# Doubling steps through four corners of the array, and every third low half of the projection's weights by GpSimd

## The chip, the cores and the metric

The kernel runs on one core of one Trainium2 chip. The metric is the device time of one execution in microseconds, as the median of several runs. The profile was taken of one more execution, and all rows below are from it.

## The reference, cut to what matters

One layer of an encoder on 256 tokens of width 2048, in float32. `h = rms_norm(x)` is projected by `w_in` (2048 x 7296) into the inputs of three mixers; their outputs go through `w_out`, then follows an MLP with `w_up` and `w_down` (width 8192). The mixer that the change touches is the RWKV-7 one, 12 heads of width 64 in two directions:

```
z = h @ w_in                       # 57 tiles of 128 columns
...
state = state * w + sa (x) bb + v (x) k      # one step per token, forward and backward
y = state . r
```

The kernel computes this recurrence in 4 chunks of 64 tokens. Within a chunk it needs the inverse of a 64 x 64 triangular matrix I - A for each head, direction and chunk. It builds the inverse by doubling: blocks of size 1 are joined to blocks of size 2, then 4, 8, 16, 32 and 64. One level computes P = A Z (masked to the blocks off the diagonal) and then Z + Z P.

## The kernel before, in words

**The float32 matmuls.** Each weight half (128 x 1024 floats, 512 KB) is fetched by SyncE into `raw` (a ring of 4, `fetch(h)`), rounded by ScalarE into `w_hi` (`hi(h)`, L1066), and VectorE takes the rest, `w_lo = raw - w_hi` (`lo(h)`, L614; both rings have 3 places). TensorE multiplies three times (L1398: hi x hi, L1399: hi x lo, L1400: lo x hi). Eight "depths" (one depth is these three matmuls of 128 x 256) use up one half; the projection has 912 depths and 114 halves. `fetch(h)` waits until the low half h-4 is done; `lo(h)` waits for `hi(h)` and for the matmuls of half h-3.

**The order of the work.** The RWKV mixer runs in 6 turns (a turn is a pair of heads). Each engine writes out the same sequence, `stage_a`: `products` (5 gaps), then five levels (`level(t, p, n, ...)`, 2 gaps each), so 15 gaps in a turn. Into each gap go the next 5 or 6 depths of the projection on TensorE (`DONE` lists how many depths are done before each gap), and on ScalarE and VectorE the halves that come due by the same list: `hi(h)` 2 depths and `lo(h)` 5 depths after the place in the ring is wanted back. The turns hold depths 336 to 840. Steps of the turn before (`chunk`) and preparations of the turn behind (`feed`, `tilde`) are threaded in between: `steps`, `between`, `behind`.

**A level.** Two directions d = 0 and 1, four chunks m, two heads e. The heads lie on partitions 0 to 63 and 64 to 127. `make_p(d)` does 8 matmuls of 64 x 64 into bank 4 + d (L1502), `make_q(d)` 8 more (L1514). Each matmul is two instructions in the trace, so `make_p(0)` and `make_p(1)` together are "x32", and so are the two `make_q`; I call such 32 instructions a block. Each matmul takes its operands from head e's partitions and writes to the same partitions, so a block uses two corners of the array, those on its diagonal. VectorE answers `make_p` with `take_p` (L763, mask into `p1s`) and `make_q` with `take_q` (L772, add into `zd`) and `transposed` (L653, into `zt`). In each level `make_p(d)` waits for `zd_ready` of its direction, and `make_q(d)` for `zt_ready` and `p1_ready` of its.

**The small steps that the rows name.** L1569 and L1577 are the four and four matmuls of `chunk`'s `u()`: the first four write to the partitions that they read from (the corners on the diagonal), the second four write to the other head's partitions (the other two corners). L1424 is the `lora` product. L1458 are `key_products` at a turn's start, which need the banks that L716 reads. L660 to L662 normalise `kkn` (`between` of level 1). L694 to L701 are `queries` and `keys`; L678 to L686 are `sums`.

**GpSimd in the turns.** It has no gaps. In turns 0 to 4 it does `bonus_and_keys` (from level 2 on): for d = 0 L516 and L519, then for d = 1 L516, and L519 only after VectorE's `keys(0)` (it waits for `tilde_ready`, L701), then L523 and L524. In each turn but the first it does `decay_state` twice (L545). Later it squares the MLP's activations (L570).

Of the kernel before, what the change touches and what calls it, by code (L numbers as in the profile page):

```python
# [8 lines left out]
ALU = mybir.AluOpType  # L9
ACT = mybir.ActivationFunctionType  # L10
F32 = mybir.dt.float32
# [4 lines left out]
T = 256  # L16
# [13 lines left out]
C = 64  # L30
NC = T // C
# [62 lines left out]
LAST_GAP = len(DONE) - 2  # L94
HI_LAG, LO_LAG, DRAIN_LAG, SHIFT_LAG = 2, 5, 2, 6


# [73 lines left out]
def layer(nc, x, pre_mix_g, w_in, na_rpb, rw_mu_prev, rw_mu_next, rw_w0, rw_w2, rw_a0, rw_a2, rw_k_k, rw_k_a,  # L171
          rw_r_k, rw_g2, rw_lnx_g, rw_lnx_b, w_out, post_mix_g, pre_mlp_g, w_up, w_down, post_mlp_g,
          cst_d, late_d, decay_d, out):
    with ExitStack() as ctx:
# [124 lines left out]
        def late_const(name):  # L299
# [31 lines left out]
            "vec_t", "vec_ready", "coef_ready",  # L331
            "hi_half", "lo_half", "gemm_half", "bank_free", "pad_free", "zs_ready",
            "lora_done", "lora_free", "wd_ready", "quarter_done", "kk_sqd", "kk_summed", "kk_root", "kk_ready",
# [21 lines left out]
        def run(pieces):  # L355
            for piece in pieces:
                piece()
# [76 lines left out]
        def _(sp):  # L434
# [18 lines left out]
            def fetch(h):  # L453
                if h >= RAW:
                    sp.wait_ge(s["lo_half"], h - RAW + 1)
# [45 lines left out]
        def _(pool):  # L501
# [4 lines left out]
            pool.dma_start(a2s, rw_a2.rearrange("l d r c -> (l d r) c")).then_inc(s["lora_in"], 16)  # L506

            def feed(t):
                return [nothing] * 5
# [17 lines left out]
            def products(t, p, steps):  # L527
                if t == RW_CT - 1:
                    pool.wait_ge(s["kb_ready"], 2 * RW_CT)
                    pool.wait_ge(s["tilde_ready"], 2 * RW_CT)  # L530
                    pool.dma_start(g2s, rw_g2[0]).then_inc(s["g2_in"], 16)
                run(steps)

            def level(t, p, n, steps, between, behind):
                run(steps)
                run(between)
                run(behind)

# [9 lines left out]

            stage_a(nothing, feed, tilde, products, level, chunk, STARTS)

# [23 lines left out]
        def _(dve):  # L574
# [64 lines left out]
            def gap():  # L639

                done = DONE[at["gap"]]
                while at["shift"] < RW_GROUPS and KT * (group_tiles(at["shift"])[-1] + 1) + SHIFT_LAG <= done:
                    shift(at["shift"])
                    at["shift"] += 1
                while at["lo"] < OUT_H and (at["gap"] == LAST_GAP or HALF_KT * (at["lo"] - SPLIT + 1) + LO_LAG <= done):
                    lo(at["lo"])
# [59 lines left out]
            def products(t, p, steps):  # L706
# [14 lines left out]
                def first_inverse(d):  # L721
                    dve.wait_ge(s["bm_ready"], 4 * t + (2 * d + 2))
                    for e in range(2):
                        h = slice(e * C, e * C + C)
                        last = dve.tensor_tensor(p1s[h, d * NC:(d + 1) * NC],
                                                 bms[p][h, (2 * d + e) * NC:(2 * d + e + 1) * NC, h],
                                                 off[h, 0].unsqueeze(1).broadcast_to([C, NC, C]), ALU.mult)
# [5 lines left out]
                    transposed(zd, zt, d, "zd_ready")  # L733

# [23 lines left out]
            def level(t, p, n, steps, between, behind):  # L758
# [8 lines left out]
                def take_q(d):  # L767
# [3 lines left out]
                    if n < len(LEVELS) - 1:  # L771
                        dve.tensor_tensor(zd[:, half], q_ps, zd[:, half], ALU.add).then_inc(s["zd_ready"], 1)  # L772
                        dve.wait_ge(s["zd_ready"], 10 * t + (2 * (n + 1) + d + 1))
                        transposed(zt, zd, d, "zt_ready")
# [595 lines left out]
        def _(pe):  # L1370
# [22 lines left out]
            def depth(dst, h, kt):  # L1393
                at = (kt % HALF_KT) * P
                if kt % HALF_KT == 0:
                    pe.wait_ge(s["lo_half"], h + 1)
                wh, wl = w_hi[:, h % SPLIT, at:at + P], w_lo[:, h % SPLIT, at:at + P]
# [98 lines left out]
            def level(t, p, n, steps, between, behind):  # L1496
                def make_p(d):
                    pe.wait_ge(s["zd_ready"], 10 * t + (2 * n + d + 1))
                    for m in range(NC):
                        for e in range(2):  # L1500
                            h = slice(e * C, e * C + C)
                            last = pe.matmul(bank[4 + d][h, m * C:(m + 1) * C], bms[p][h, (2 * d + e) * NC + m, h],  # L1502
                                             zd[h, d * NC + m], start=True, stop=True)
                    last.then_inc(s["p1_done"], 1)

                def make_q(d):
                    pe.wait_ge(s["zt_ready"], 10 * t + (2 * n + d + 1))
                    pe.wait_ge(s["p1_ready"], 10 * t + (2 * n + d + 1))

                    by, of = (zt, p1s) if n < len(LEVELS) - 1 else (p1s, zt)  # L1510
                    for m in range(NC):
                        for e in range(2):
                            h = slice(e * C, e * C + C)
                            last = pe.matmul(bank[4 + d][h, T + m * C:T + (m + 1) * C], by[h, d * NC + m],  # L1514
                                             of[h, d * NC + m], start=True, stop=True)
                    last.then_inc(s["q_done"], 1)

                make_p(0)
                make_p(1)
                run(steps[:1])  # L1520
                gap()
                run(between)
                make_q(0)
                make_q(1)
                run(steps[1:])
                gap()
                run(behind)
# [188 lines left out]
            def rows(n, lhs_hi, lhs_lo, first=False, final=False):  # L1716
# [10 lines left out]

                pe.wait_ge(s["lo_half"], 2 * n + 1)
                if final:
                    pe.wait_ge(s["lo_half"], 2 * n + 2)  # L1730
                    part(0, 0).then_inc(s["quarter_done"], 1)
# [4 lines left out]
                for j in range(2):  # L1736
                    if j:
                        pe.wait_ge(s["lo_half"], 2 * n + 2)
                    part(1, j)
# [42 lines left out]
```

## Time and profile before

| what | us |
|---|---|
| median of 3 runs (1446.81 to 1453.39) | 1447.47 |
| the profiled execution | 1448.14 |
| its span, first to last instruction | 1446.3 |
| TensorE busy | 1378.7 (95%) |
| VectorE busy | 823.6 (57%) |
| ScalarE busy | 633.0 (44%) |
| GpSimd busy | 128.2 (9%) |

The span is what lies between the first and the last instruction; 1.8 us of the execution's time lie around it. The turns take the stretch from about 146 to 487 us. An engine's busy share says little by itself: matmuls overlap, and what counts is which wait ends last in a stretch.

### The profile page before, as it was taken

Reading aid. Unit: us, or ns where it says so; the run is one execution under the profiler, and the core shown is the slowest. Engines: PE = TensorE matmul, PEld = TensorE weight load, DVE = VectorE, ACT = ScalarE, POOL = GpSimd, SP = SyncE. Lnnn points to the kernel's source line nnn. Section 1 sums busy time; section 2 is a strip of 40 time slices with the busy share of each in tenths; the row PEclk is TensorE's granted clock in tenths of the full one; section 3 lists DMA queues with packets and bytes.
Section 4 is the critical chain, followed back from the end, with each engine's and each line's share of the span. In section 5 each row is a group of like instructions: output and inputs, shape, how many; then the busy total and the mean of one; then the engine's idle time right before and its main releaser. Section 6 shows DMA issues by size and latency. Waiting matters only on the chain.

```text
span 1446.3 us, 27251 instructions
## 1 busy us (share of the span) xinstructions
PE 1378.7 (95%) x11565; PEld 1244.4 (86%) x11565; DVE 823.6 (57%) x1170; ACT 633.0 (44%) x949; POOL 128.2 (9%) x119
## 2 busy tenths in 40 slices
PE   6999999999999989699799999999999999999997
PEld 6999888888988876488599999999998888888885
DVE  5566787787877664544744444444445555455455
ACT  5555444444443333433634444443434444444443
POOL 0000021011111131100011111111110000000000
PEclk9999999999999989799899999999999999999999
DMA  8666333333333820157286666666665665666663
GB/s 248 177 173 176 103 103 99 94 89 104 103 103 101 204 75 1 44 207 235 83 231 180 185 182 183 185 181 187 179 188 189 196 195 190 193 195 194 191 196 123
DMA packets 285756, 226.61 MB, mean 157 GB/s; under 512 B 15236, under 2 KB 263300, under 8 KB 284740
## 3 DMA queue, kind: packets, MB, share of 16 engines
q1 hardware_dynamic: 285168, 223.64, 51.9%
q8 instruction: 91, 1.49, 0.4%
q0 software_dynamic: 240, 1.18, 0.3%
q14 instruction: 29, 0.24, 0.0%
q10 hardware_dynamic: 228, 0.07, 0.0%
HBM read 222.76 MB, written 2.10 MB: 155 GB/s over the span
## 4 chain that ended last, share of the span: by engine, by line
PE 84%; DVE 7%; ACT 4%; issue 3%; DMA 1%; SPq 1%; ACTq 0%; POOL 0%; DVEq 0%
PE psum L1724 30%; PE psum L1398 15%; PE psum L1399 14%; PE psum L1400 14%; PE psum L1502 2%; PE psum L1514 2%; DVE w_lo L614 1%; ACT w_hi L1066 1%; SPq L477 1%; PE psum L1647 1%; PE psum L1644 1%; PE psum L1424 1%; DMA raw<-in_w_in 1%; DVE arena L716 1%; PE psum L1559 0%
## 5 line engine op out<-in xcount | busy, mean ns | idle before, releaser
L614 DVE TENSOR_TENSOR w_lo<-raw,w_hi 128x1024 fp32r<-128x1024 f32 x402 | 493.4, 1230 | 476.7 <-ACT w_hi L1066 475.9
L1066 ACT ACTIVATE w_hi<-raw 128x1024 fp32r<-128x1024 f32 x402 | 424.7, 1060 | 506.5 <-PE psum L1400 260.2
L1398 PE MATMUL psum<-act_hi,w_hi 128*128 128x256 f32 x1936 | 559.7, 289 | 6.9 <-DVE w_lo L614 5.4
L1399 PE MATMUL psum<-act_lo,w_hi 128*128 128x256 f32 x1936 | 547.5, 283 | 0.0
L1400 PE MATMUL psum<-act_hi,w_lo 128*128 128x256 f32 x1936 | 547.3, 283 | 0.0
L1398 PEld LDWEIGHTS psum<-act_hi,w_hi 128*128 128x128 f32 x1936 | 370.6, 191 | 16.4 <-DVE w_lo L614 5.2
L1399 PEld LDWEIGHTS psum<-act_lo,w_hi 128*128 128x128 f32 x1936 | 370.9, 192 | 0.1
L1400 PEld LDWEIGHTS psum<-act_hi,w_lo 128*128 128x128 f32 x1936 | 370.8, 192 | 0.0
L1724 PE MATMUL psum<-w_hi,act_hi 128*128 128x512 f32 x640 | 198.6, 392 | 2.6 <-issue 2.6
L1724 PE MATMUL psum<-w_hi,act_lo 128*128 128x512 f32 x640 | 198.0, 391 | 0.0
L1724 PE MATMUL psum<-w_lo,act_hi 128*128 128x512 f32 x640 | 197.9, 391 | 0.0
L1724 PEld LDWEIGHTS psum<-w_hi,act_hi 128*128 128x128 f32 x640 | 120.6, 189 | 28.3 <-issue 3.2
L1724 PEld LDWEIGHTS psum<-w_lo,act_hi 128*128 128x128 f32 x640 | 120.9, 189 | 25.2
L1724 PEld LDWEIGHTS psum<-w_hi,act_lo 128*128 128x128 f32 x640 | 120.7, 189 | 25.2
L570 POOL TENSOR_TENSOR arena<-arena 128x512 f32<-128x512 f32 x32 | 50.7, 1583 | 445.7 <-ACT arena L1346 445.7
L1502 PEld LDWEIGHTS psum<-arena 64*64 64x64 f32 x960 | 30.5, 134 | 7.6 <-issue 4.0
L763 DVE TENSOR_TENSOR arena<-psum,cst 128x256 f32<-128x256 f32 x60 | 24.8, 422 | 21.4 <-PE psum L1502 20.2
L1502 PE MATMUL psum<-arena 64*64 64x64 f32 x960 | 34.8, 221 | 0.4 <-DVE arena L772 0.3
L1514 PE MATMUL psum<-arena 64*64 64x64 f32 x960 | 34.4, 221 | 0.0
L1514 PEld LDWEIGHTS psum<-arena 64*64 64x64 f32 x960 | 30.3, 134 | 4.0
L772 DVE TENSOR_TENSOR arena<-psum,arena 128x256 f32<-128x256 f32 x48 | 19.4, 405 | 20.6 <-PE psum L1514 20.4
L516 POOL TENSOR_TENSOR arena<-arena 128x256 f32<-128x256 f32 x12 | 12.0, 1001 | 214.7 <-ACT arena L1165 214.7
(195 smaller groups left out, 933.6 us busy)
## 6 DMA issues: line engine op xcount, KB each, us to landing
raw<-in_w_up SPq DMA_DIRECT2D x128, 512.0 KB, 4.0
raw<-in_w_down SPq DMA_DIRECT2D x128, 512.0 KB, 3.6
raw<-in_w_in SPq DMA_DIRECT2D x114, 512.0 KB, 4.1
raw<-in_w_out SPq DMA_DIRECT2D x32, 512.0 KB, 4.2
arena<-in_x SPq DMA_DIRECT2D x2, 1024.0 KB, 6.2
arena<-in_na_rpb SPq DMA_DIRECT2D x16, 128.0 KB, 4.9
arena<-in_x SPq DMA_DIRECT2D x1, 2048.0 KB, 8.5
out_x<-arena SPq DMA_DIRECT2D x4, 512.0 KB, 2.7
```

Of the source, the lines that this page charges most:

```text
L477: sp.dma_start(dst, src).then_inc(s["bias_in"], 16)
L570: pool.tensor_tensor(dst, relu_t[:, q % 2], relu_t[:, q % 2], ALU.mult).then_inc(s["relu_free"], 1)
L614: dve.tensor_tensor(w_lo[:, h % SPLIT], raw[:, h % RAW], w_hi[:, h % SPLIT].bitcast(F32), ALU.subtract).then_inc(s["lo_half"], 1)
L763: dve.tensor_tensor(p1s[:, half], bank[4 + d][:, 0:T].rearrange("p (n t) -> p n t", t=C), off[:, n + 1].unsqueeze(1).broadcast_to([P, NC, C]),
L772: dve.tensor_tensor(zd[:, half], q_ps, zd[:, half], ALU.add).then_inc(s["zd_ready"], 1)
L1066: act.activation(w_hi[:, h % SPLIT], raw[:, h % RAW], ACT.Copy).then_inc(s["hi_half"], 1)
L1398: pe.matmul(dst, wh, act_hi[:, kt], start=kt == 0, stop=False)
L1399: pe.matmul(dst, wh, act_lo[:, kt], start=False, stop=False)
L1400: last = pe.matmul(dst, wl, act_hi[:, kt], start=False, stop=kt == KT - 1)
L1502: last = pe.matmul(bank[4 + d][h, m * C:(m + 1) * C], bms[p][h, (2 * d + e) * NC + m, h], zd[h, d * NC + m], start=True, stop=True)
L1514: last = pe.matmul(bank[4 + d][h, T + m * C:T + (m + 1) * C], by[h, d * NC + m], of[h, d * NC + m], start=True, stop=True)
L1724: last = pe.matmul(bank[4 * t + 2 * j + b], lhs[:, tokens], w[:, h % SPLIT, b * 512:(b + 1) * 512], start=start, stop=stop)
```

## The change

**Four corners.** For direction 1 the 64 x 64 matrices of `p1s` and `zt` are kept on the other head's partitions in levels 0 to 3. So `make_p` of direction 1 writes crosswise and `make_q` of direction 1 reads there and writes back: its matmuls lie in the two corners off the diagonal. `make_p` and `make_q` each become one loop, over chunks, then directions, then heads. Each waits once, for both directions. The last level (n = 4) has the new order, and all of its matmuls stay on the diagonal. `crossed` takes the place of `transposed` for direction 1 at four places of a turn: two transposes of 64 partitions instead of one of 128.

**Low halves by GpSimd.** Of the halves whose place comes free within the turns every third (h = 47, 50, 53 ... 104, 20 in all) has its low half computed by GpSimd, with a gap function of its own: `lo(h)` comes at the gap at which `hi(h)` comes. VectorE leaves these out. Whoever waited for low halves now waits for two counts, `lo_half` and `lo_pool`: SyncE's `fetch`, TensorE's `depth` and `rows`.

```
+TURNS_FROM, TURNS_TO = DONE[DENSE_GAPS], DONE[DENSE_GAPS + RW_CT * TURN_GAPS]
+POOL_LO = [h for h in range(OUT_H) if h % 3 == 2 and TURNS_FROM < half_wanted(h) < TURNS_TO]
...
+        def lo_ready(eng, h):
+            of_dve, of_pool = lo_counts(h)
+            if of_dve:
+                eng.wait_ge(s["lo_half"], of_dve)
+            if of_pool:
+                eng.wait_ge(s["lo_pool"], of_pool)
...
+            def lo(h):
+                pool.wait_ge(s["hi_half"], h + 1)
+                pool.wait_ge(s["gemm_half"], h - SPLIT + 1)
+                pool.tensor_tensor(w_lo[:, h % SPLIT], raw[:, h % RAW], w_hi[:, h % SPLIT].bitcast(F32),
+                                   ALU.subtract).then_inc(s["lo_pool"], 1)
...
             def level(t, p, n, steps, between, behind):
-                run(steps)
+                run(steps[:1])
+                gap()
                 run(between)
+                run(steps[1:])
+                gap()
                 run(behind)
...
+            def crossed(dst, src, name):
+                half = slice(NC, 2 * NC)
+                for e in range(2):
+                    h, o = slice(e * C, e * C + C), slice((1 - e) * C, (2 - e) * C)
+                    last = dve.transpose(dst[o, half].rearrange("p n t -> p (n t)"),
+                                         src[h, half].rearrange("p n t -> p (n t)"))
+                last.then_inc(s[name], 1)
...
+                def tiles():
                     for m in range(NC):
+                        for d in range(2):
+                            for e in range(2):
+                                h, o = slice(e * C, e * C + C), slice((1 - e) * C, (2 - e) * C)
+                                yield m, d, e, h, o if d and crossing else h
+
+                def make_p():
+                    pe.wait_ge(s["zd_ready"], 10 * t + (2 * n + 2))
+                    for m, d, e, h, to in tiles():
+                        last = pe.matmul(bank[4 + d][to, m * C:(m + 1) * C], bms[p][h, (2 * d + e) * NC + m, h],
+                                         zd[h, d * NC + m], start=True, stop=True)
```

## Rows read from the trace of the kernel before

**Rows 1.** The page's first line.

```profile
span 1446.3 us, 27251 instructions
```

**Rows 2.** Busy time by windows: window, length, then PE, PEld, DVE, ACT, POOL, clock, DMA.

```profile
155.00:485.00 330.00, 320.41 (x4625) 291.31 (x4625) 252.91 (x508) 142.03 (x252) 43.60 (x51) 1.00 0.36 102
800.00:900.00 100.00, 100.00 (x836) 100.00 (x835) 42.91 (x35) 41.16 (x44) 14.40 (x9) 1.00 0.64 184
```

**Rows 3.** Waits from 160 to 485 us: us in total, times, longest.

```profile
PE psum L1398 <- DVE w_lo L614: 3.5, 4, 1.1
PE psum L1458 <- DVE arena L716: 2.4, 3, 0.8
```

**Rows 4.** Timeline of TensorE, a block and the depth behind it: start, duration.

```profile
246.92 1.15 PE L1514 MATMUL psum<-arena 64*64 64x64 f32 x32
247.99 0.39 PE L1398 MATMUL psum<-act_hi,w_hi 128*128 128x256 f32 x1
```

**Rows 5.** Timeline of TensorE where diagonal (L1569) and other corners (L1577) meet.

```profile
284.62 0.23 PE L1569 MATMUL psum<-arena 64*64 64x64 f32 x2
284.63 0.27 PE L1577 MATMUL psum<-arena 64*64 64x64 f32 x2
284.67 0.28 PE L1569 MATMUL psum<-arena 64*64 64x64 f32 x3
...
284.80 0.28 PE L1577 MATMUL psum<-arena 64*64 64x64 f32 x3
285.01 0.38 PE L1398 MATMUL psum<-act_hi,w_hi 128*128 128x256 f32 x1
```

**Rows 6.** VectorE by lines: transposes and instructions on 64 partitions, min/median/max ns.

```profile
L653 DVE STREAM_TRANSPOSE arena<-arena x60: 445/445/448, 150.1 to 477.6; 128x256 f32<-128x256 f32 x60
L725 DVE TENSOR_TENSOR arena<-arena,cst x24: 416/420/423, 148.8 to 438.0; 64x256 f32<-64x256 f32 x24
```

**Rows 7.** VectorE's low halves from 155 to 485 us, by line.

```profile
L614 DVE TENSOR_TENSOR w_lo<-raw,w_hi x62: 1181/1224/1267, 154.6 to 483.6; 128x1024 fp32r<-128x1024 f32 x62
```

**Rows 8.** GpSimd's operations with two inputs, 256 and 512 wide: timeline, and by line.

```profile
298.04 0.74 POOL L516 TENSOR_TENSOR arena<-arena 128x256 f32<-128x256 f32 x1
...
L556 POOL TENSOR_TENSOR arena<-arena x8: 1271/1298/2269, 502.9 to 513.5; 128x512 f32<-128x512 f32 x8
```

**Rows 9.** VectorE's timeline: the same operations, alone and beside GpSimd.

```profile
239.97 1.22 DVE L678 TENSOR_TENSOR_SCAN arena<-cst,arena 128x256 f32<-128x256 f32 x1
...
296.01 0.68 DVE L678 TENSOR_TENSOR_SCAN arena<-cst,arena 128x256 f32<-128x256 f32 x1
...
507.67 2.27 DVE L614 TENSOR_TENSOR w_lo<-raw,w_hi 128x1024 fp32r<-128x1024 f32 x1
```

**Rows 10.** Timelines of VectorE, GpSimd and TensorE, end of turn 1 (levels 3 and 4).

```profile
247.65 0.42 DVE L772 TENSOR_TENSOR arena<-psum,arena 128x256 f32<-128x256 f32 x1 [1.05 <-PE psum L1514]
...
251.44 0.42 DVE L701 TENSOR_TENSOR arena<-arena 128x256 f32<-128x256 f32 x1
...
252.00 0.74 POOL L519 TENSOR_TENSOR arena<-arena 128x256 f32<-128x256 f32 x1 [9.41 <-DVE arena L701]
...
253.77 0.59 POOL L524 COPY arena<-arena 128x256 f32<-128x256 f32 x1
...
252.60 0.28 PE L1398 MATMUL psum<-act_hi,w_hi 128*128 128x256 f32 x1
```

**Rows 11.** Timelines of ScalarE, VectorE and TensorE, turn 2, before level 2.

```profile
283.81 1.28 ACT L1142 ACT_TABLE_LOAD   x1 [3.20 <-PE psum L1424]
...
291.67 0.39 DVE L772 TENSOR_TENSOR arena<-psum,arena 128x256 f32<-128x256 f32 x1
...
292.07 0.33 PE L1502 MATMUL psum<-arena 64*64 64x64 f32 x4
```

**Rows 12.** A long wait of TensorE, and the window (as rows 2) behind its end.

```profile
532.89 1.19 PE L1644 MATMUL psum<-arena 128*128 128x512 f32 x1 [4.16 <-DVE arena L885]
...
532.00:549.00 17.00, 14.54 (x29) 7.41 (x30) 9.04 (x17) 6.81 (x17) 4.21 (x4) 0.51 0.00 1
```

More of the change, by code:

```diff
@@ L506, in _, with gap @@
             pool.dma_start(a2s, rw_a2.rearrange("l d r c -> (l d r) c")).then_inc(s["lora_in"], 16)
+            at = {"gap": 0, "lo": 0}
+            def lo(h):
[3 more added lines that the diff above has]
+                                   ALU.subtract).then_inc(s["lo_pool"], 1)
+            def gap():
+                done = DONE[at["gap"]]
+                while at["lo"] < len(POOL_LO) and half_wanted(POOL_LO[at["lo"]]) + HI_LAG <= done:
+                    lo(POOL_LO[at["lo"]])
+                    at["lo"] += 1
+                at["gap"] += 1
             def feed(t):
@@ L531, in products @@
                     pool.dma_start(g2s, rw_g2[0]).then_inc(s["g2_in"], 16)
-                run(steps)
+                for step in steps:
+                    step()
+                    gap()
             def level(t, p, n, steps, between, behind):
-                run(steps)
+                run(steps[:1])
+                gap()
                 run(between)
+                run(steps[1:])
+                gap()
                 run(behind)
@@ L547, in chunk @@
                 return decay_state if n in (1, 2) else nothing, nothing, nothing
-            stage_a(nothing, feed, tilde, products, level, chunk, STARTS)
+            stage_a(gap, feed, tilde, products, level, chunk, STARTS)
+            assert at["lo"] == len(POOL_LO)
             pool.wait_ge(s["bias_in"], 16 * ROWS * ROWS)
@@ L773, in take_q @@
                         dve.wait_ge(s["zd_ready"], 10 * t + (2 * (n + 1) + d + 1))
-                        transposed(zt, zd, d, "zt_ready")
+                        if d and n < len(LEVELS) - 2:
+                            crossed(zt, zd, "zt_ready")
+                        else:
+                            transposed(zt, zd, d, "zt_ready")
                     else:
@@ L1496, in level @@
             def level(t, p, n, steps, between, behind):
-                def make_p(d):
-                    pe.wait_ge(s["zd_ready"], 10 * t + (2 * n + d + 1))
+                crossing = n < len(LEVELS) - 1
+                def tiles():
                     for m in range(NC):
[L1500 to L1516, printed above, removed]
@@ L1518, in level @@
-                make_p(0)
-                make_p(1)
+                        for d in range(2):
[7 more added lines that the diff above has]
+                                         zd[h, d * NC + m], start=True, stop=True)
+                        if m == NC - 1 and e == 1:
+                            last.then_inc(s["p1_done"], 1)
@@ new lines, in make_q @@
+                def make_q():
+                    pe.wait_ge(s["zt_ready"], 10 * t + (2 * n + 2))
+                    pe.wait_ge(s["p1_ready"], 10 * t + (2 * n + 2))
+                    by, of = (zt, p1s) if crossing else (p1s, zt)
+                    for m, d, e, h, at in tiles():
+                        last = pe.matmul(bank[4 + d][h, T + m * C:T + (m + 1) * C], by[at, d * NC + m],
+                                         of[at, d * NC + m], start=True, stop=True)
+                        if m == NC - 1 and e == 1:
+                            last.then_inc(s["q_done"], 1)
@@ L1520, in level @@
+                make_p()
                 run(steps[:1])
@@ L1522, in level @@
                 run(between)
-                make_q(0)
-                make_q(1)
+                make_q()
                 run(steps[1:])
```

28 lines of the change are left out of this document (19 added, 9 removed).

## The prediction, written before the changed kernel ran

> **What bounds the kernel now.** I read the page first, then busy time by windows, then the waits of the turns, then the timelines of single places. Nothing outside the turns is touched except for one more wait per half, so the turns are where to look. In 155 to 485 us TensorE is busy 320.4 of 330 us, VectorE 252.9 (77%), GpSimd 43.6 (13%) [rows 2]. TensorE is the bound, and it waits for VectorE at few places: 3.5 us for low halves and 2.4 us for L716 in all six turns [rows 3]. So time taken off TensorE in the turns counts, as long as VectorE, whose chains lie close behind, keeps up; and a late low half stops TensorE outright.
>
> **Four corners: what TensorE saves.** A block of 32 instructions takes 1.07 us up to the next depth (246.92 to 247.99) [rows 4]: two go at a time, 16 slots of some 0.06 us, and the pipe's end. Can four go at a time? L1569 and L1577 are 16 instructions over the four corners. L1577 starts 0.01 us behind the first L1569 and long before the last, and the next depth starts 0.39 us after the first (284.62 to 285.01) [rows 5]. Another 16 of that kind need 4 slots more, 0.23 us, so a block in four corners is 0.62 us, and the saving 0.45 us. Levels 0 to 3 have a p block and a q block each: 4 x 2 x 6 turns = 48 blocks, 48 x 0.45 = **-21.6 us**. The 12 blocks of level 4 stay on the diagonal: 0. Bounds: 48 x 0.24 (half the corners' effect, if a block mixes worse than L1569 and L1577 do) = -11.5, and all 16 slots down to 8 with nothing lost, 48 x 0.48 = -23. I take -21.6, the nearest rows.
>
> The Trainium skill speaks against this: "TensorE: Matmul & The Clock Gate", Part 3 (packing small matmuls), says that a weight load overlaps with running matmuls only when its row group is another one. Two of the four corners share their rows. By that rule the block would stay near 1.07 us and this term would be 0. Rows 5 show corners with shared rows at work together, so I go by the rows and keep the rule as a rival.
>
> **VectorE: what it gains and pays.** 20 low halves leave it: 20 x 1.22 = -24.5 us [rows 7]. `crossed` has two transposes where there was one, 4 per turn, so 24 more. None on 64 partitions is in the trace: at least 0.42 (another operation of 64 x 256), at most 0.45 (the whole transpose) [rows 6]; 24 x 0.45 = +10.8 us. All of them stand behind the `zd` that the next p block needs, so they delay only `zt`, for which a q block comes more than 1 us later. Net -14 us, hidden, since VectorE is not the bound.
>
> **GpSimd: what a low half costs.** Two inputs of 256 take it 0.74 us, of 512 1.27 to 1.30 [rows 8]; so 0.53 us per 256 more, and about 0.2 + 4 x 0.53 = 2.3 us for 1024 (a straight line; no row has that width; bounds 2.2 and, beside a busy VectorE, 3.5). It is idle 87% of the turns, so 20 x 2.3 = 46 us find room. But each holds something that VectorE wants too: L678 took 0.68 us alone and 1.22 beside GpSimd, L614 2.27 instead of 1.22 [rows 9, 7]. So one wait of up to 2.3 us for VectorE per low half, where it wants two inputs from SBUF. By my estimate from its lines about 30% of its work is of that kind apart from L614; 20 x 0.3 x half of 2.3 = 7 us on VectorE, which leaves it 7 us ahead of before. On the end I take 0.
>
> **The low halves that come late.** GpSimd works in its program's order, and in turns 0 to 4 that order has a wait in it: between level 2 and the end of level 3 it stands at L519 for `keys(0)` (9.41 us in turn 1) [rows 10]. A low half written behind it can't start before. This hits gap 12 of a turn, where h = 62 (turn 1) and h = 83 (turn 3) lie; h = 104 has the same place in turn 5, where L519 is not run. I counted the places of all 20: h = 47, 68, 89 at gap 5, 59, 80, 101 at 7, 50, 71, 92 at 9, 53, 74, 95 at 14, 56, 77, 98 at 3, 65 and 86 at 1. These find GpSimd free at least 5 us before their use. For h = 62: the q block of level 3 starts at 246.92, `keys(0)` ends 4.9 us later, L524 (GpSimd's last of its chain) ends at 254.36, 7.4 us after the block's start, and the low half is ready at 7.4 + 2.3 = 9.7, with 0.1 for the signal 9.8. TensorE wants it for the depth that began at 252.60 [rows 10], after the change 0.45 sooner, thus at 5.2. **It waits 4.6 us**, and 0.2 more if L686 holds GpSimd back: 4.8. Turn 3 has the same rows 116 us later. 2 x 4.8 = **+9.6 us**. Nothing gives that back, since TensorE is the bound on both sides of it. Bounds: 2 x 3.5 and 2 x 6.
>
> **The clock.** After a wait of 4.16 us the granted clock was 0.51 (the 1.2 GHz level) in 532 to 549 us, and TensorE had been busy before [rows 12]. 4.8 us is as long. At the lower level a few microseconds of dense depths take twice their time; I put 3 us on a fall that ends 6 us after work resumes (the lower bound is 0, no fall; the upper 8, as long as in rows 12). For two waits I take one fall: **+3 us**.
>
> **Where VectorE is just in time.** Before level 2 of turn 2 L772 is done at 292.06 and the p block starts at 292.07 [rows 11]: no slack. The chain goes back by L660 to L662 and ScalarE to L1424, and only two shortened blocks lie before that (-0.9), but four before the p block (-1.8). So 0.9 us of the saving is lost there, in turns 0, 2 and 4; in turns 1 and 3 level 3 is the tight place, by half of that. Also a merged `make_p` waits for both directions. 3 x 0.9 + 2 x 0.5 + 0.3 = **+4 us** (bounds 1 and 8). At the ends of turns 0, 2 and 4 TensorE waits 1.9 us already [rows 3]; there one low half leaves (-1.2), one transpose comes (+0.45), the block's end is nearer (+0.45): **-0.5 us** in all.
>
> **The second wait per half.** From h = 47 on TensorE and SyncE wait for two counts. In 800 to 900 us TensorE is busy 100.00 of 100 us with a wait at each half and two at each new bank [rows 2], so it costs nothing as long as both have come. From h = 47 to the last, 401, there are 355 halves; 0.02 us for each would be 7 us. I take 0.
>
> **The sum.** -21.6 + 9.6 + 3 + 4 - 0.5 = -5.5 us. The profiled execution took 1448.14 us (span 1446.3 [rows 1]), so 1442.6; the median lies 0.7 lower. **Predicted: 1442 us**, a change of -0.4%.
>
> **The rivals.** *A. The two waits come, the clock stays:* 1439. For it: dense work on both sides. *B. They don't come, or last under 1 us,* as `keys(0)` would have to be 4 us earlier: 1442 - 12.6 + 2 = 1431. Against it: the order of the program forces GpSimd to stand there; for it only that VectorE has one low half less in front of L772. *C. GpSimd holds up VectorE where TensorE waits for it, slower than before.* Place: the ends of the turns, where VectorE works for 13 to 20 us without a pause, and the tight places of rows 11. If each low half costs VectorE the full 2.3 us, 46 us stand against 24.5 saved, with the transposes +32 us on VectorE; two thirds of it on TensorE's waits is +21: 1442 + 21 = 1463. It decides from 0.3 us per low half on (20 x 0.3 = 6): above, the change is a loss. Against it: the level's own chain (L763, L772, L653) reads PSUM or one input and isn't held. *D. The corners that share rows don't overlap:* the first term is 0, the +4 goes too: 1447.5 + 9.6 + 3 = 1460. The saving must be under 0.3 us per block to lose. *E. The tight places cost less,* 1 us instead of 4, and the clock stays: 1436.
>
> **How the numbers follow.** A change of 0.5% (7.2 us, so 1440.2 and 1454.7) is about what the measurement tells from none. Forecast with one or two falls of the clock (1441 to 1447): 0.38. A: 0.20. B: 0.11. C: 0.14, half of it beyond 1454.7. D: 0.04. E: 0.13. Faster takes B, E, three quarters of A and a little of the forecast: 0.42. Slower: D and half of C, 0.11. Within: 0.47. Range: B's 1431 at one end and a mild C (0.5 us per low half, +10) at the other: 1430 to 1453.
>
> **What would show it.** In the changed trace: p and q blocks of levels 0 to 3 0.6 us long (L1502 and L1514's successors), those of level 4 still 1.07; TensorE idle 4 to 5 us before L1398, released by GpSimd's low half, twice, 116 us or a little less apart, in turns 1 and 3 only; GpSimd's low halves 2.3 us; the clock below 1 in the windows right behind. The prediction is wrong if the blocks stay at 1 us, if L1398 waits for GpSimd in other turns too, or if TensorE's waits for VectorE in the turns grow past 15 us.

## The result, and the profile after

| | median of the runs, us | range | ratio to before, 95% interval |
|---|---|---|---|
| before | 1448.38 | 1446.81 to 1453.39 | |
| changed | 1467.95 | 1464.14 to 1470.16 | 1.0126 [1.0093, 1.0159] |

The change makes the kernel 1.3% slower; 1442 (range 1430 to 1453) was predicted. The profiled execution took 1468.17 us. Its page begins, and in its part 5 has, these lines (last columns: busy us, mean ns | idle before it, releaser):

```profile
span 1466.3 us, 27838 instructions
...
L655 DVE TENSOR_TENSOR w_lo<-raw,w_hi 128x1024 fp32r<-128x1024 f32 x382 | 471.3, 1237 | 468.1 <-ACT w_hi L1124 467.1
...
L533 POOL TENSOR_TENSOR w_lo<-raw,w_hi 128x1024 fp32r<-128x1024 f32 x20 | 48.5, 2423 | 186.3 <-ACT w_hi L1124 186.3
```

The code has moved down by some 40 to 65 lines: the p block is L1567 now (L1502 before), the q block L1578 (L1514), the first matmul of a depth L1456 (L1398), VectorE's low half L655 (L614), its `keys` L752 (L701), its scan L729 (L678). GpSimd's low half is L533, the crossed transposes L697.

**Where the time went, by stages.** By the starts of the first matmuls of depths 336 and 840 the turns last 352.0 us, against 338.5 before: +13.5. The attention stage behind them (from depth 911 to 912) lasts 198.4, against 192.1: +6.3. The rest agrees within 0.3 us. Windows of the turns in the changed kernel, to be read beside [rows 2], the second being the first stretch behind a late low half:

```profile
155.00:485.00 330.00, 298.53 (x4420) 268.34 (x4419) 248.99 (x495) 138.73 (x248) 89.70 (x70) 0.96 0.34 96
...
256.60:260.00 3.40, 3.40 (x39) 3.06 (x39) 0.23 (x1) 0.06 (x1) 0.00 (x0) 0.50 0.54 153
```

TensorE is idle 31.5 of the 330 us (9.6 before), and its mean clock is 0.96, not 1.00. Its waits from 140 to 520 us, as in [rows 3]:

```profile
PE psum L1456 <- POOL w_lo L533: 7.2, 2, 3.7
PE psum L1567 <- DVE arena L827: 6.0, 6, 1.6
PE psum L1611 <- DVE arena L886: 4.9, 4, 1.2
PE psum L1456 <- DVE w_lo L655: 4.2, 4, 1.5
PE psum L1516 <- DVE arena L767: 3.6, 3, 1.2
```

The first line is the two late low halves. The others are waits for VectorE, 18.7 us together where the prediction put its own bound at 15: the p block waits for the step before it on VectorE (`take_q`, L827), which before the change it did once, by 0.3 us.

**The blocks** answer to [rows 4]. A p or q block of levels 0 to 3, then a p block of level 4, each with the depth behind it:

```profile
188.07 0.69 PE L1578 MATMUL psum<-arena 64*64 64x64 f32 x32
188.70 0.39 PE L1456 MATMUL psum<-act_hi,w_hi 128*128 128x256 f32 x1
...
250.19 1.15 PE L1567 MATMUL psum<-arena 64*64 64x64 f32 x32
251.27 0.39 PE L1456 MATMUL psum<-act_hi,w_hi 128*128 128x256 f32 x1
```

From 188.07 to 188.70 are 0.63 us, from 250.19 to 251.27 are 1.08. This part came as forecast.

**GpSimd and VectorE at the same time.** A timeline of turn 0 where h = 53 is due (start, duration, engine; in brackets idle time and releaser):

```profile
196.89 1.05 ACT L1124 ACTIVATE w_hi<-raw 128x1024 fp32r<-128x1024 f32 x1
...
197.83 0.42 DVE L751 SCALAR_TENSOR_TENSOR arena<-arena 128x256 f32<-128x256 f32 x1
198.01 2.47 POOL L533 TENSOR_TENSOR w_lo<-raw,w_hi 128x1024 fp32r<-128x1024 f32 x1 [2.84 <-ACT w_hi L1124]
198.17 2.60 DVE L752 TENSOR_TENSOR arena<-arena 128x256 f32<-128x256 f32 x1
...
200.63 0.36 PE L1456 MATMUL psum<-act_hi,w_hi 128*128 128x256 f32 x1
```

`keys` (L752) takes 2.60 us where it takes 0.42 else. GpSimd's subtraction began 0.16 us before it, and `keys` ends 0.29 us after the subtraction, at 200.77. The same at two more places, the scan L729 in turn 2 and L713 (the norm of `kkn`) in turn 3, where the trace has both start at once:

```profile
301.12 2.49 POOL L533 TENSOR_TENSOR w_lo<-raw,w_hi 128x1024 fp32r<-128x1024 f32 x1 [14.12 <-ACT w_hi L1124]
301.28 2.87 DVE L729 TENSOR_TENSOR_SCAN arena<-cst,arena 128x256 f32<-128x256 f32 x1
...
354.49 2.68 DVE L713 SCALAR_TENSOR_TENSOR arena<-arena,small 128x256 f32<-128x256 f32 x1
354.50 2.39 POOL L533 TENSOR_TENSOR w_lo<-raw,w_hi 128x1024 fp32r<-128x1024 f32 x1 [8.35 <-ACT w_hi L1124]
```

Going through the 20 low halves one by one, 11 of them hold one of VectorE's operations up: h = 53, 59, 71, 74, 80, 92, 95 and 104 by 1.6 to 2.2 us, h = 50, 65 and 86 by 0.8 to 1.4. Each of these operations reads two inputs from SBUF. The other nine hold nothing. What reads one input, or one from PSUM, isn't held: four of the crossed transposes (L697) and seven of `take_q`'s additions (L827, one input in PSUM) start beside a subtraction, and none of either takes longer than usual in the whole run (min/median/max ns):

```profile
L697 DVE STREAM_TRANSPOSE arena<-arena x48: 439/440/443, 154.3 to 485.1; 64x256 f32<-64x256 f32 x48
...
L827 DVE TENSOR_TENSOR arena<-psum,arena x48: 385/400/426, 166.0 to 491.3; 128x256 f32<-128x256 f32 x48
```

**A late low half**, h = 62 in turn 1, answers to [rows 10]:

```profile
247.58 0.69 PE L1578 MATMUL psum<-arena 64*64 64x64 f32 x32
...
250.97 0.42 DVE L752 TENSOR_TENSOR arena<-arena 128x256 f32<-128x256 f32 x1
...
253.29 0.59 POOL L559 COPY arena<-arena 128x256 f32<-128x256 f32 x1
253.85 2.52 POOL L533 TENSOR_TENSOR w_lo<-raw,w_hi 128x1024 fp32r<-128x1024 f32 x1
...
256.51 0.46 PE L1456 MATMUL psum<-act_hi,w_hi 128*128 128x256 f32 x1 [3.54 <-POOL w_lo L533]
```

TensorE waits 3.54 us here and 3.66 at h = 83 (380.46), and nowhere else for GpSimd. The last matmul shown takes 0.46 us, the three behind it 0.41 to 0.42 where they take 0.28 before the wait, and the granted clock in the window 256.60 to 260.00 is 0.50, the 1.2 GHz level.

**The attention stage** has more time at the lower level. Two windows of the changed kernel, then the second one's counterpart before the change:

```profile
546.80:577.50 30.70, 29.12 (x75) 18.02 (x74) 11.28 (x22) 9.53 (x34) 4.22 (x4) 0.50 0.00 0
611.60:635.50 23.90, 14.15 (x45) 11.15 (x46) 10.58 (x22) 7.08 (x20) 0.48 (x1) 0.50 0.18 59
```

```profile
600.60:617.70 17.10, 9.96 (x33) 7.93 (x32) 6.65 (x15) 5.43 (x14) 0.00 (x0) 0.50 0.08 28
```

With the short stretches it is 68.3 us at 0.50 against 47.8, and half of the 20.5 more would be 10; 6.3 us came, as part of it is time in which TensorE waits anyway.

### The profile page after: what moved, and what is told of

It is laid out like the page before. It is cut to its first block, busy times and chain, and to the rows that moved or that the text cites. A ratio compares the mean times of both kernels' runs of the same rounds, so it can differ in the third digit from the quotient of the medians.

```text
span 1466.3 us, 27838 instructions
## 1 busy us (share of the span) xinstructions
PE 1377.3 (94%) x11565; PEld 1238.3 (84%) x11565; DVE 828.2 (56%) x1174; ACT 634.5 (43%) x949; POOL 176.7 (12%) x139
## 3 DMA queue, kind: packets, MB, share of 16 engines
q0 software_dynamic: 240, 1.18, 0.2%
## 4 chain that ended last, share of the span: by engine, by line
PE 81%; DVE 11%; ACT 4%; issue 3%; POOL 1%; ACTq 0%; DVEq 0%; POOLq 0%
PE psum L1787 29%; PE psum L1456 15%; PE psum L1457 14%; PE psum L1458 14%; DVE w_lo L655 2%; PE psum L1578 1%; PE psum L1710 1%; PE psum L1707 1%; PE psum L1567 1%; DVE arena L752 1%; DVE arena L827 1%; DVE arena L712 1%; PE psum L1752 1%; DVE arena L767 1%; DVE arena L729 1%
## 5 line engine op out<-in xcount | busy, mean ns | idle before, releaser
L655 DVE TENSOR_TENSOR w_lo<-raw,w_hi 128x1024 fp32r<-128x1024 f32 x382 | 471.3, 1237 | 468.1 <-ACT w_hi L1124 467.1
L1456 PE MATMUL psum<-act_hi,w_hi 128*128 128x256 f32 x1936 | 563.7, 291 | 16.2 <-POOL w_lo L533 7.2
L1456 PEld LDWEIGHTS psum<-act_hi,w_hi 128*128 128x128 f32 x1936 | 373.6, 193 | 27.0 <-issue 8.1
L533 POOL TENSOR_TENSOR w_lo<-raw,w_hi 128x1024 fp32r<-128x1024 f32 x20 | 48.5, 2423 | 186.3 <-ACT w_hi L1124 186.3
L818 DVE TENSOR_TENSOR arena<-psum,cst 128x256 f32<-128x256 f32 x60 | 22.7, 419 | 23.9 <-PE psum L1567 23.6
L1236 ACT ACTIVATE arena<-arena 64x256 f32<-64x256 f32 x24 | 8.7, 408 | 52.5 <-DVE arena L752 52.5
L1567 PEld LDWEIGHTS psum<-arena 64*64 64x64 f32 x960 | 19.8, 137 | 13.4 <-DVE arena L827 8.3
L1567 PE MATMUL psum<-arena 64*64 64x64 f32 x960 | 24.0, 227 | 6.0 <-DVE arena L827 6.0
L827 DVE TENSOR_TENSOR arena<-psum,arena 128x256 f32<-128x256 f32 x48 | 19.4, 405 | 17.9 <-PE psum L1578 17.6
L1077 DVE TENSOR_TENSOR act_lo<-arena,act_hi 128x256 fp32r<-128x256 f32 x64 | 27.4, 428 | 2.1 <-ACT act_hi L1414 2.1
```

Source lines behind the costliest of these rows:

```text
L533: pool.tensor_tensor(w_lo[:, h % SPLIT], raw[:, h % RAW], w_hi[:, h % SPLIT].bitcast(F32), ALU.subtract).then_inc(s["lo_pool"], 1)
L655: dve.tensor_tensor(w_lo[:, h % SPLIT], raw[:, h % RAW], w_hi[:, h % SPLIT].bitcast(F32), ALU.subtract).then_inc(s["lo_half"], 1)
L818: dve.tensor_tensor(p1s[:, half], bank[4 + d][:, 0:T].rearrange("p (n t) -> p n t", t=C), off[:, n + 1].unsqueeze(1).broadcast_to([P, NC, C]),
L1077: dve.tensor_tensor(u_lo[:, m % U_RING], u[:, m], u_hi[:, m % U_RING].bitcast(F32), ALU.subtract).then_inc(s["ulo_done"], 1)
L1456: pe.matmul(dst, wh, act_hi[:, kt], start=kt == 0, stop=False)
L1567: last = pe.matmul(bank[4 + d][to, m * C:(m + 1) * C], bms[p][h, (2 * d + e) * NC + m, h], zd[h, d * NC + m], start=True, stop=True)
```

## The experiments

A table of all of them first, as each is read against the others. "Turns" is the time from depth 336 to depth 840, "idle" TensorE's idle time from 145 to 500 us, "half" the time in the turns with the granted clock at 0.50, all from the profiled execution.

| kernel | median, us | ratio to before [95%] | turns | idle | half |
|---|---|---|---|---|---|
| before | 1448 | | 338.5 | 10.6 | 0 |
| changed | 1467.95 | 1.0126 [1.0093, 1.0159] | 352.0 | 31.8 | 23.9 |
| e14, changed again | 1468.08 | 1.0122 [1.0099, 1.0144] | 351.9 | 31.8 | 23.9 |
| e1, corners only | 1444.23 | 0.9970 [0.9952, 0.9987] | 334.5 | 22.3 | 10.2 |
| e2, GpSimd only | 1462.42 | 1.0092 [1.0057, 1.0127] | 350.5 | 17.8 | 6.8 |
| e3, none in the late places | 1452.77 | 1.0029 [1.0008, 1.0049] | 345.1 | 24.4 | 27.3 |
| e5, one write each | 1444.93 | 0.9975 [0.9957, 0.9993] | 334.5 | 20.0 | 17.1 |
| e6, three writes each | 1452.17 | 1.0027 [1.0012, 1.0043] | 342.3 | 24.4 | 23.9 |
| e7, seven clear places | 1445.64 | 0.9988 [0.9978, 0.9998] | 337.3 | 21.8 | 17.1 |
| e8, seven held places | 1451.25 | 1.0024 [1.0008, 1.0041] | 340.3 | 26.5 | 10.2 |
| e9, two late, corners | 1455.15 | 1.0051 [1.0034, 1.0068] | 348.2 | 28.6 | 27.3 |
| e15, two late, diagonal | 1457.42 | 1.0055 [1.0036, 1.0073] | 348.2 | 16.7 | 6.8 |
| e10, merged, diagonal | 1450.56 | 1.0014 [0.9995, 1.0033] | 340.9 | 12.7 | 0 |
| e11, one transpose | 1440.41 | 0.9946 [0.9925, 0.9967] | 329.9 | 17.6 | 10.2 |
| e12, norm later | 1447.97 | 1.0006 [0.9987, 1.0025] | 337.9 | 25.4 | 10.2 |
| e13, norm and sums later | 1444.5 | 0.9964 [0.9941, 0.9987] | 331.4 | 21.6 | 3.4 |

A check on the reading: if the corners save 21.6 us of work, a kernel's turns should differ from before by -21.6 (where it has corners), plus its further idle time, plus half of its time at 0.50. For the changed kernel that is -21.6 + 21.2 + 12.0 = +11.6 (measured +13.5); e1 -21.6 + 11.7 + 5.1 = -4.8 (-4.0); e3 +5.9 (+6.6); e7 -1.8 (-1.2); e8 -0.6 (+1.8); e9 +10.1 (+9.7); e15 +6.1 + 3.4 = +9.5 (+9.7). All agree within 2.5 us, and so do the others of the table. The last three columns come from one execution each, which need not lie at the median: it took 1458.28 us in e2, 1448.46 in e8, 1458.57 in e9 and 1458.40 in e10.

### e1 and e2: each half of the change alone

```
# e1, in the changed kernel
-POOL_LO = [h for h in range(OUT_H) if h % 3 == 2 and TURNS_FROM < half_wanted(h) < TURNS_TO]
+POOL_LO = []
# e2: the changed kernel with before's make_p, make_q, p1s and transposed
```

> The four corners alone: no low half goes to GpSimd. Theory H (GpSimd's low halves are what costs: TensorE waits for two late ones, they hold up VectorE's operations with two inputs from SBUF, and the longer waits let the clock fall): the blocks keep their saving of some 20 us, a part is lost where VectorE is just in time, the clock stays at 1.00 in the turns; 1448 - 20 + 8 = about 1436, and GpSimd's share of the change is then +32. Theory C (the corners are at fault: one merged wait for both directions, two transposes for one, and short packed blocks behind which the clock falls): 1450 or more, with several falls of the clock in the turns. Theory W (the second wait per half on TensorE): the projection's turns are as in theory C's best case and the stretches outside the turns shorten against the changed kernel by several us.

> The 20 low halves by GpSimd alone, the blocks as before on the diagonal. Theory H: no saving, two late waits of 3 to 4.6 us, VectorE held by some 18 us in the turns of which TensorE feels a third, clock falls behind the two waits: 1448 + 8 + 6 + 4 = 1466, turns 15 to 20 us longer than before. Theory C: TensorE comes later to each wait than with the corners, so only the two late waits show: 1448 + 8 = 1456 or less.

The corners alone are 0.3% faster, the low halves alone 0.9% slower; together 1.3%. So adding GpSimd's low halves to the corners costs 1467.95 - 1444.23 = 23.7 us. Waits of e1's TensorE from 155 to 500 us show where the corners' gain of 21.6 went:

```profile
PE psum L1456 <- DVE w_lo L655: 5.5, 4, 1.6
PE psum L1567 <- DVE arena L827: 4.9, 5, 1.6
PE psum L1516 <- DVE arena L767: 3.8, 3, 1.3
PE psum L1611 <- DVE arena L886: 2.5, 2, 1.2
```

TensorE now reaches places before VectorE does. The mechanism was foreseen; the size was not. In e2 the same 11 low halves hold VectorE up, by about as much, yet TensorE's idle time is only 7.2 us above that of before, and 6.3 of these are the two late waits. With the blocks on the diagonal the relief of VectorE and its room make up for nearly all of the holds; with the corners they don't.

### e3 and e9: the late places left out, and alone

```
# e3
+POOL_LO = [h for h in POOL_LO if h not in (62, 83, 104)]
# e9
+POOL_LO = [h for h in POOL_LO if h in (62, 83)]
```

> The whole change, but the low halves 62, 83 and 104 (gap 12 of a turn) stay with VectorE; 17 are left to GpSimd. My late-wait term: TensorE's waits of 3.5 and 3.7 us for GpSimd are gone, and the two falls of the clock behind them: 1468 - 7 - 4 = 1457. If the holds on VectorE are what costs, most of the 13.6 us in the turns stays; if the two late ones were the main cause, the kernel comes down to 1448 or less.

> The four corners, and only the low halves 62 and 83 by GpSimd, those that TensorE waits for. The waits themselves are 3.5 and 3.7 us in the changed kernel; with no clock effect 1444 + 7 = 1451, with a fall of the clock behind each 1455 to 1458. The changed kernel less the one without these (62, 83, 104) was 15 us; if that is theirs, 1459.

On top of e1, the two late ones alone cost 10.9 us (turns +13.7) and the other 17 alone 8.5 (turns +10.6). All 20 together cost 17.5 in the turns, less than the sum of 24.3. The idle times add up (6.3 and 2.1 us over e1 each alone, 9.5 together); what doesn't is the time at 0.50, 17.1 us more than in e1 in each of e3 and e9, but only 13.7 more in the changed kernel. In e9 the two waits are 7.1 us and half of the 17.1 is 8.6, so the clock is as dear as the waits, in this execution. Only 6.8 of the 17.1 lie right behind the two waits; the rest came elsewhere in the turns, in places where e1 had kept its clock.

```profile
PE psum L1457 <- POOL w_lo L534: 7.1, 2, 3.5
```

### e5 and e6: GpSimd's place taken by an operation that only writes

```
# e5; e6 does it three times one behind the other
-pool.tensor_tensor(w_lo[:, h % SPLIT], raw[:, h % RAW], w_hi[:, h % SPLIT].bitcast(F32), ALU.subtract)
+pool.memset(w_lo[:, h % SPLIT].bitcast(F32), 0.0)
```

Both leave the value of these 20 low halves out.

> The whole change, but for the 20 halves GpSimd writes zeros to the low half and reads nothing (the low part of these 20 halves is left out of the product). The waits, the order and the relief of VectorE are those of the changed kernel; only the reading of two inputs is gone and the operation is shorter. If GpSimd's reading of SBUF is what holds VectorE: VectorE's keys and scans go back to 0.42 and 0.68 us, the late waits shrink to 1 or 2 us, and the time is that of the corners alone or a little less: 1434 to 1440. If something else in the new order holds VectorE (one more engine in the ring of waits): it stays above 1455.

> The whole change, but GpSimd writes zeros to the low half three times in a row instead of subtracting: some 2.9 us without reading SBUF (one such write took 0.95 us), longer than the subtraction's 2.42 (the low part of these 20 halves is left out of the product). The two late waits stay or grow to about 4 us each, so this keeps my late-wait term and takes away only the reading. Theory H1 (a GpSimd operation that reads two inputs holds VectorE's operations with two inputs for its whole length): L752's, L713's, L729's successors are back at 0.42, 0.48 and 0.68 us, the time is 1444 + 8 for the late waits + 3 for the clock = about 1455. Theory H2 (it is the length of GpSimd's operation, whatever it does): the holds stay, 1468 or more.

By line, the memsets (the view counts the last of each three) and VectorE's `keys` in e6, then `keys` in the changed kernel (min/median/max ns):

```profile
L536 POOL MEMSET w_lo<- x20: 951/952/955, 166.5 to 480.1; 128x1024 f32 x20
...
L754 DVE TENSOR_TENSOR arena<-arena x12: 418/420/422, 109.3 to 438.1; 128x256 f32<-128x256 f32 x12
```

```profile
L533 POOL TENSOR_TENSOR w_lo<-raw,w_hi x20: 2365/2392/2542, 164.2 to 487.0; 128x1024 fp32r<-128x1024 f32 x20
...
L752 DVE TENSOR_TENSOR arena<-arena x12: 418/420/2609, 109.0 to 445.3; 128x256 f32<-128x256 f32 x12
```

And e6's timeline at h = 53, the place at which `keys` was held above:

```profile
198.19 1.96 POOL L534 MEMSET w_lo<- 128x1024 f32 x2 [2.81 <-ACT w_hi L1126]
...
198.37 0.42 DVE L754 TENSOR_TENSOR arena<-arena 128x256 f32<-128x256 f32 x1
```

Three writes keep GpSimd 2.9 us for each low half, longer than the subtraction, and hold nothing: `keys` starts 0.18 us into them and stays at 0.42. So it isn't GpSimd's work as such, but its reading (of two inputs; a GpSimd operation with one input wasn't tried). With the waits for GpSimd grown to 9.2 us in 5 places e6 is 16 us faster than the changed kernel, 9.7 us of it in the turns. In e5, with one short write each, the turns are as long as in e1 (334.5): TensorE waits 4.0 us for GpSimd, but its waits for `key_products` (L1516 in e1, 3.8 us) are gone and those for VectorE's low halves are 2.4 us instead of 5.5. So the relief of VectorE is worth some 7 us of waiting when nothing is held. The Trainium skill ("SBUF — State Buffer", the section on the two separate sides) has this rule: VectorE and GpSimd share one pair of ports under an exclusive lock for a whole instruction, and a VectorE operation with two inputs from SBUF needs it only against a GpSimd operation that reads. These runs agree, with 2.60 us beside the subtraction and 0.42 beside the memsets.

### e7 and e8: seven that hold nothing, seven that hold

```
# e7
+POOL_LO = [h for h in POOL_LO if h in (47, 56, 68, 77, 89, 98, 101)]
# e8
+POOL_LO = [h for h in POOL_LO if h in (53, 59, 71, 74, 80, 92, 95)]
```

> The four corners, and only the seven low halves by GpSimd beside which no VectorE operation was lengthened in the changed kernel: 47, 56, 68, 77, 89, 98, 101. If only the holds and the late waits cost: 1444, as the corners alone, or up to 4 us less, since VectorE has seven low halves less. If any low half on GpSimd costs about the same (24 us by 20): 1444 + 8 = 1452.

> The four corners, and only the seven low halves by GpSimd beside which an operation of VectorE's chain took 1.6 to 2.2 us longer: 53, 59, 71, 74, 80, 92, 95 (14.3 us of holds in all, 8.6 us of relief). If the holds cost where they fall on a chain that TensorE waits for: 1444 + 6 to 10 = 1450 to 1454, with L1516's, L1567's and L1611's waits longer than in the kernel with the seven clear ones. If VectorE's slack takes them up: 1444.

The two kernels do the same number of low halves on GpSimd; `keys` by line in e7, then in e8:

```profile
L753 DVE TENSOR_TENSOR arena<-arena x12: 415/420/422, 109.5 to 432.3; 128x256 f32<-128x256 f32 x12
```

```profile
L753 DVE TENSOR_TENSOR arena<-arena x12: 412/421/2600, 109.1 to 434.3; 128x256 f32<-128x256 f32 x12
```

The intervals of the ratios don't overlap. The medians differ by 5.6 us, the turns by 3.0, for 14.3 us of holding (seven times 1.6 to 2.2), with 4.7 us more of TensorE's idle time. So a held microsecond on VectorE cost 0.2 to 0.4 us in the end. e7, where nothing is held, still isn't faster than e1: the 7 x 1.22 us that leave VectorE at these places don't bring anything. The places where the relief counted in e5 aren't among them: here TensorE's wait for VectorE at `key_products` stays at 3.6 us.

### e10 to e13: why the corners save 4 us and not 21.6

```
# e10, on e1: all tiles on the diagonal, merged loops and waits kept
+to = h
# e11, on e1, at both places of direction 1
-crossed(zd, zt, "zd_ready")
+transposed(zd, zt, d, "zd_ready")
# e12, on e1; e13 also puts tl[0] from between to behind
-between = [(), (norm,), (tl[0],), (), (tl[3],)]
-behind = [(lora_first,), (lora_second,), (), tl[1:3], tl[4:6]]
+between = [(), (), (tl[0],), (), (tl[3],)]
+behind = [(lora_first,), (lora_second, norm), (), tl[1:3], tl[4:6]]
```

In e11 direction 1 takes the other head's numbers; the instructions are otherwise the same.

> The kernel before with one part of the corners: each p and q block is one loop over chunks, directions and heads with one wait for both directions, and everything stays on the diagonal (blocks of 1.07 us, one transpose). It prices the merged wait. If the merged wait is a cost of its own: 1450 to 1453, with TensorE waits for L772's successor of several us where the kernel before had 0.3. If it isn't: 1448, and the corners' lost saving comes from VectorE being just in time for a TensorE that comes sooner.

> The four corners alone, but direction 1 is transposed in one instruction as before (it leaves out the change of partitions, so the numbers of direction 1 are of the wrong head). It prices the 24 added transposes, 10.6 us on VectorE. If they are hidden, as I had it: within 1 us of the corners alone, 1444. If VectorE's chain feels them: down to 1438, with L1516's and L1456's waits shorter.

> The four corners alone, with VectorE's normalisation (L711 to L714, 2.6 us) behind take_q of level 1 instead of in front of it. In the corners alone TensorE waits at that place in turns 0, 2 and 4 (1.6, 0.9, 0.9 us, and 1.2 us twice behind it), and the clock fell behind two of them. If these waits are what ate the corners' saving: -5 to -6 us for the waits and -2 for the clock, about 1437. If the wait only moves to the next place: 1442 to 1444.

> As the run before, and the first sums (with ScalarE's and GpSimd's part of them) behind level 2 instead of within it, where turns 1 and 3 wait 1.0 and 0.5 us, and 0.65 behind each. If all the waits in the turns are of this kind: another -2 to -4 us, 1434. Against it: the keys of level 3 then come later, and their chain ends at the next turn's start, where TensorE already waits 1.2 us: then 1440 or more.

The merged waits cost some 2 us (e10; turns +2.4, and the interval of the ratio holds no change too). The second transpose costs 3.8 us by the medians (e11 against e1) and 4.6 in the turns, of the 10.8 that I had called hidden. e12 removes one wait and gets more back behind it: in it the p block waits 7.3 us for VectorE and the depths 7.7 for low halves, in e1 4.9 and 5.5. At 1447.97 it is 3.7 us slower than e1, above both values that were expected. e13 does shorten the turns by 3.1 us, but five of its ten runs were 1440.4 to 1442.0 and five 1447.0 to 1449.1; the profiled one is of the second kind and has 8.7 us more in the attention stage than e1, with a stretch of 30.7 us at 0.50 where e1 has 17.1. No kernel that computes the layer is clearly better than the corners alone.

### e14 and e15: the clock

```
# e14: the changed kernel once more, unaltered
# e15, on e2
+POOL_LO = [h for h in POOL_LO if h in (62, 83)]
```

> The changed kernel once more, in more runs. Its turns took 13.5 us longer than before in the profile, but the whole 19.6; the other 6.3 lie between 540 and 738 us, in stages that the change does not touch, at a lower granted clock (0.5 for 30.7 and 23.9 us there, 17.1 and 17.1 before). If that belongs to the change, every run is at 1464 to 1470. If it comes and goes with the run, as the same 8 us do in other kernels here (1440.5 and 1448 in one of them), some runs are near 1460.

> The kernel before with the low halves 62 and 83 by GpSimd and nothing else: late waits on TensorE with blocks on the diagonal. The same two with the corners cost 11 us (1444.2 to 1455.2), though they are 7 us of waiting. If the clock falls at short waits only in kernels with packed blocks: here 2 x 3.8 of waiting and 2 falls of 3.4 us at half the clock, 3.4 us: 1448 + 7.5 + 3.5 = 1459 at most, with the clock at 1.00 elsewhere in the turns. If it falls at short waits here too: 1462.

e14 answers whether the 6 us of the attention stage were a chance of one execution. Four of its five runs are at 1467.6 to 1468.4, one at 1462.1 with a mean clock of 0.973 against 0.965 or 0.966, as one of the first four was (1464.14, 0.972). By the clock they come with most runs of this kernel, not with all. What makes a kernel fall for 30.7 and not 17.1 us there isn't settled: the profiled executions of e10 and e13 fell so too, with quite other turns.

e15 answers how dear a late wait is without the corners: two waits, 6.3 us, then two stretches of 3.4 us at 0.50, and +9.7 us in the turns. Windows over the turns and behind the first wait:

```profile
155.00:500.00 345.00, 328.27 (x4668) 298.11 (x4666) 256.23 (x512) 143.51 (x255) 48.76 (x53) 0.99 0.37 100
257.10:260.50 3.40, 3.40 (x36) 3.28 (x32) 2.55 (x6) 0.00 (x0) 0.00 (x0) 0.50 0.52 151
```

## Why the prediction was wrong, step by step

**The corners' blocks: right.** 0.63 us was measured where 0.62 was put, level 4 unchanged at 1.08, and the balance above closes with -21.6 in all eleven kernels that have them. Rival D falls: corners that share their rows do overlap. By the rule of the Trainium skill that the prediction cites ("TensorE: Matmul & The Clock Gate", Part 3) the block would have stayed near 1.07 us; the measured 0.63 doesn't agree with it.

**The late low halves: right in place, a little too dear.** Turns 1 and 3 only, 124 us apart; 3.54 and 3.66 us, 7.2 together instead of 9.6. `keys(0)` ended 3.8 us after the q block's start and not 4.9 (251.39 - 247.58), as VectorE has the 1.18 us of this low half no longer in front of it. The 0.2 us for a held operation didn't come.

**"On the end I take 0" for GpSimd's holds: this step failed.** I had 7 us of holding on VectorE, set it against the 24.5 us that VectorE saves, and so let it vanish. What happened is rival C's mechanism, which had 0.14. Three things were wrong in it. First, the probability: I took 30% as the chance that a low half meets an operation with two inputs, as though they met at random. But GpSimd is released by ScalarE's `hi(h)`, which has its fixed place in the gap (it ends at 197.94 for h = 53), just when VectorE begins the same gap's chain; the same race recurs in turn after turn (`keys` in turns 0, 2 and 4), and 11 of 20 hold. Second, I wrote that the low halves "find GpSimd free at least 5 us before their use". GpSimd was free, but the low half can't begin before `hi(h)`: for h = 53 that is at 198.01, and its use at 200.63 comes 0.15 us after its end. Third, I set a gain spread over 330 us against a loss at a few tight places. e7 shows seven places where the gain is worth nothing, e8 what the placed loss costs: +7.0 us over e1 for seven of them. Where the gain does count, at the turns' starts (e5), the hold takes it away again. For all 20 the reading costs 16 us by the medians, 9.7 of it in the turns (e6 against the changed kernel).

**"VectorE just in time", +4: mis-sized, and the largest miss.** TensorE's idle time grew by 11.7 us in e1, with neither late nor held low halves. I had counted only the one tight place that I had looked at in each turn ([rows 11]) and nothing for the transposes; e11 gives these 3.8 us. To it comes the clock: three stretches of 3.4 us at 0.50 that were not there before, 5.1 us. So the corners bring 4 us, not 17.6, which is a miss of 13.6 in the turns. On GpSimd's side, from e1 to the changed kernel, the turns grew by 17.5 where 9.6 + 3 - 0.5 = 12.1 was put, a miss of 5.4.

**The ends of turns 0, 2 and 4, -0.5: wrong sign.** [rows 3] has 2.4 us of waiting there, not 1.9, and by its own parts the term is 3 x -0.3 = -0.9. In the changed kernel these waits are 3.6 us (L1516), as three of the low halves that were to relieve them hold `keys` instead (h = 53, 74, 95); in e5, where they don't, the waits are gone.

**The clock, +3: mis-sized.** In the turns of the changed kernel 23.9 us pass at the lower level, half of it 12.0. I had one fall in view, behind a late wait. Both late waits have one (3.4 us from 256.6, and 6.8 from 379.5 on, inside the wait), and there are four more behind waits for VectorE of 0.9 to 1.6 us, three of the four with a second wait of 0.35 to 0.89 us some 0.7 us away. Outside the turns it brought 6.3 us more, a stage that I had declared untouched. Of this nothing was in the sum.

**The second wait per half, 0: right.** Outside the turns and the attention stage the two kernels agree within 0.3 us, though every half up to the last, 401, waits for two counts.

**The sum.** From before to after: corners -21.6, idle +21.2 (7.2 late, the rest VectorE: 11.7 in e1 already, 2.3 more), clock in the turns +12.0, 1.9 unexplained, attention stage +6.3: +19.8, against 19.6 between the medians. For the step from e1 to the changed kernel, 23.7 us: idle +9.5, clock +6.9, attention stage 198.4 against 190.9, +7.5; together 23.9. Rival C's 1463 came nearest, but with its late waits cheaper, its holds cheaper, and the clock dearer than it had them.

## What to carry to other kernels

Giving an idle engine some work is free only if each piece's own start, not the engine's idleness, lies clear of what it shares with others: find for every piece what releases it, and look what the neighbour does in that very microsecond. Don't offset a loss that falls on a tight place with a gain spread over the rest: the gain counts only where it stands ahead of a tight place itself. And work taken off the bounding engine counts only up to the next place where the engine behind it is just in time: count all of these places before, with the idle time and the slower clock that follow from them, and not one for each turn.

## What the runs showed of the hardware that was not expected

- A subtraction of two 128 x 1024 inputs on GpSimd (2.37 to 2.54 us) makes a VectorE operation with two inputs from SBUF, a scan too, wait to its end (0.42 us becomes 2.60); three memsets over the same tile (0.95 us each) don't, and a transpose (0.44) or an addition with one input in PSUM (0.39 to 0.42) isn't held by either.
- 32 instructions of 64 x 64 over the four corners take 0.63 us, on the diagonal 1.08.
- Kernels whose blocks all lie on the diagonal (before, e2, e10, e15) went to the lower clock in the turns only behind waits of 3.1 us and more (0, 2, 0 and 2 times), though they have waits of 1.0 to 1.1 us too. With the corners packed it fell behind waits of 0.9 to 1.6 us as well (3 times in e1 and in e8, 5 in e7), several times two of them close together, as 0.89 and 1.24 us before 408.2 in e1. Why is open; that these waits are longer and more may be all of it.
- The same work in the attention stage began with a stretch of 13.7 or 17.1 us at the lower level in most kernels and with one of 30.7 in the changed kernel, e10 and e13, where the stage is 6 to 9 us longer. The stretch begins some 47 us behind depth 840, and the kernels differ only ahead of that, the second wait per half aside. e13's ten runs fall into two groups 5 us apart, so it may be chance of the execution as well; what decides isn't known.
